# A change to the first attention of a two-block transformer kernel: item order, head-pair values, and who loads and masks the bias

## The reference, cut to what matters

```python
def neighbourhood_attention(x, w_qkv, w_o, rpb):
    qkv = (x @ w_qkv).reshape(b, rows, GRID_W, 3, N_HEADS, HEAD_DIM)   # rows = 4, GRID_W = 64
    ...
        sc = jnp.einsum('bhqd,bhrkd->bhqrk', qi, kr).astype(jnp.float32)
        sc = sc + jnp.transpose(bias, (0, 2, 1, 3))[None]
        sc = jnp.where(col_mask[:, None, :], sc, NEG_INF)
        p = jax.nn.softmax(...)
        return jnp.einsum('bhqrk,bhrkd->bhqd', p.astype(vr.dtype), vr)
    ...
    return o @ w_o
```

## Time and profile before

| what | value |
|---|---|
| median of 3 runs | 2100.27 us (2098.11 to 2106.24) |
| profiled execution, span from first to last instruction | 2099.1 us |
| TensorE busy | 1917.0 us, 91% |
| VectorE busy | 1000.8 us, 48% |
| ScalarE busy | 644.8 us, 31% |
| GpSimd busy | 217.1 us, 10% |
| mean granted TensorE clock | 0.943 |

### The profile page before, as it was taken

How to read it: one execution, slowest core, us unless ns; L and a number is a source line. 1 busy time by engine, 2 the same in 40 slices (tenths; PEclk the granted TensorE clock), 3 DMA queues, 4 the chain that set the end, 5 groups by cost and what they waited for, 6 DMA issues and landing times.

```text
span 2099.1 us, 33697 instructions
## 1 busy us (share of the span) xinstructions
PE 1917.0 (91%) x14454; PEld 1390.5 (66%) x14454; DVE 1000.8 (48%) x1382; ACT 644.8 (31%) x1004; POOL 217.1 (10%) x218
## 2 busy tenths in 40 slices
PE   6878999899997899989999779989899999999993
PEld 5757999889996899855765669874344444444440
DVE  4664554555654677756545774663122121111116
ACT  4334333544444533330033531422111111111110
POOL 0000000000000100002100014401111121121213
PEclk9878999999999999999899879989999999999996
DMA  9313555544442777546511000066998998998886
GB/s 328 101 61 114 190 188 180 168 152 153 150 151 91 263 248 250 162 150 193 160 51 43 0 13 4 3 274 269 386 381 341 379 382 347 379 371 353 329 344 256
DMA packets 191893, 438.68 MB, mean 209 GB/s; under 512 B 24208, under 2 KB 145552, under 8 KB 162448
## 3 DMA queue, kind: packets, MB, share of 16 engines
q1 hardware_dynamic: 156336, 352.02, 45.6%
q0 software_dynamic: 23040, 43.05, 6.0%
q10 hardware_dynamic: 12384, 41.69, 5.1%
HBM read 501.68 MB, written 26.21 MB: 251 GB/s over the span
## 4 chain that ended last, share of the span: by engine, by line
PE 79%; DVE 10%; DMA 4%; ACT 3%; issue 2%; SPq 0%; POOL 0%; ACTq 0%; DVEq 0%; POOLq 0%
PE psum L344 30%; PE psum L3324 15%; PE psum L3345 7%; PE psum L1538 7%; PE psum L3295 4%; PE psum L1545 2%; DMA mem<-in_exp_w_dram 2%; PE psum L2555 2%; ACT w_hi L400 1%; DMA mem<-in_na_w_qkv_dram 1%; PE psum L2539 1%; DVE w_lo L405 1%; DVE mem L3449 1%; PE psum L564 1%; PE psum L3085 1%
## 5 line engine op out<-in xcount | busy, mean ns | idle before, releaser
L405 DVE TENSOR_TENSOR w_lo<-mem,w_hi 128x2048 fp32r<-128x2048 f32 x122 | 279.3, 2291 | 264.6 <-ACT w_hi L400 262.0
L344 PE MATMUL psum<-x_hi,w_hi 128*128 128x256 f32 x1216 | 352.0, 289 | 4.5 <-DVE x_lo L551 4.5
L3324 PE MATMUL psum<-mem 128*64 128x512 f32 x1536 | 342.4, 599 | 9.5 <-DMA mem<-in_exp_w_dram 9.4
L344 PE MATMUL psum<-x_hi,w_lo 128*128 128x256 f32 x1216 | 346.1, 285 | 0.0
L344 PE MATMUL psum<-x_lo,w_hi 128*128 128x256 f32 x1216 | 345.3, 284 | 0.0
L400 ACT ACTIVATE w_hi<-mem 128x2048 fp32r<-128x2048 f32 x122 | 233.8, 1918 | 199.7 <-PE psum L344 186.1
L3324 PEld LDWEIGHTS psum<-mem 128*64 128x64 f32 x1536 | 110.6, 138 | 233.2 <-issue 214.6
L344 PEld LDWEIGHTS psum<-x_hi,w_hi 128*128 128x128 f32 x1216 | 235.8, 194 | 11.1 <-DVE w_lo L405 4.9
L344 PEld LDWEIGHTS psum<-x_lo,w_hi 128*128 128x128 f32 x1216 | 239.3, 197 | 0.7
L344 PEld LDWEIGHTS psum<-x_hi,w_lo 128*128 128x128 f32 x1216 | 238.1, 196 | 0.0
L3345 PE MATMUL psum<-mem 128*64 128x512 f32 x768 | 177.0, 603 | 1.2 <-DVE mem L3396 1.0
(11 more groups left out here) (494 smaller groups left out, 2963.4 us busy)
## 6 DMA issues: line engine op xcount, KB each, us to landing
mem<-in_exp_w_dram SPq DMA_DIRECT2D x192, 1024.0 KB, 12.5
mem<-in_dil_w_qkv_dram SPq DMA_DIRECT2D x36, 1024.0 KB, 5.3
mem<-in_ada_w_dram POOLq DMA_DIRECT2D x48, 512.0 KB, 4.7
y_rows<-mem ACTq DMA_DIRECT2D x48, 512.0 KB, 8.0
mem<-in_ffn_w_gate_dram SPq DMA_DIRECT2D x22, 1024.0 KB, 5.6
mem<-in_ffn_w_up_dram SPq DMA_DIRECT2D x22, 1024.0 KB, 5.6
mem<-in_ffn_w_down_dram SPq DMA_DIRECT2D x22, 1024.0 KB, 4.8
mem<-in_w_in_dram SPq DMA_DIRECT2D x13, 1024.0 KB, 5.6
```

What stands on the lines that cost most here:

```text
L344: ins = pe.matmul(out, lhs[a], rhs[b], start=start and k == 0, stop=stop and k == 2, **kw)
L405: dve.tensor_tensor(w_lo[n % SLOTS][:, 0, :], ring[:, n % SLOTS, :], w_hi_f[n % HI][:, 0, :], ALU.subtract).then_inc(S("w_split"), 1)
L3324: ins = pe.matmul(psum[r, up, :].rearrange("p (a n) -> p a n", a=2), xg[:, b % 2, c, x * P + 64 * e:x * P + 64 * e + 64], w_up[s][e][:, :, ...
```

## The change

- The items come in another order: head blocks 2 and 3 first get Q and K each, and then V of both.
- The units start at slots 4, 5, 7, 8, 10, 11, 13, 14, 16, 17, 18, ..., 23: one in each slot from 16 on.
- The value products of a pair of heads (two units) are made together, in 8 matmuls, in slots 8, 11, 14, 17, 22, 23, 24 and 26; their output leaves PSUM in one copy of 256 columns. The list of slots ends at 26.
- The turned probabilities have six buffers in place of two, and ScalarE copies them out of PSUM in place of VectorE.
- `lo_dve` moves from the end of a slot of the second half to the end of the next one, behind that slot's `scaled` and `biased`.
- The bias is loaded in four quarters, the first ahead of the attention, the others from ScalarE's queue after slots 1, 5 and 9, each behind a wait for the one before. The constants follow after slot 11, the gain row after slot 15, the small inputs after slot 17.
- The mask is added to the bias on GpSimd, a quarter at a time.

```diff
@@ -775,10 +775,11 @@
 
 
 
+    PT_RING = 6
     qT, kT, v_tok = alloc(KC, SEQ), alloc(KC, SEQ), alloc(NT, D)
     na_bias = alloc(HEADS, 6, GRID_W)
     na_p = alloc(2, 2, SEQ)
-    na_pT = alloc(2, 4, P)
+    na_pT = alloc(PT_RING, 4, P)
     na_s = alloc(2, 2, SEQ)
     na_max = alloc(2 * HEADS)
     na_sum = alloc(2 * HEADS)
@@ -814,10 +815,12 @@
 
         eng.wait_ge(S(f"qkv_moved{m % 2}"), m // 2 + 1)
 
-    NA_ITEMS = [(hb, kind) for hb in range(4) for kind in range(3)]
+    NA_ITEMS = [(0, 0), (0, 1), (0, 2), (1, 0), (1, 1), (1, 2), (2, 0), (2, 1), (3, 0), (3, 1), (2, 2), (3, 2)]
+    NA_AT = {item: m for m, item in enumerate(NA_ITEMS)}
     PAIRS2 = HEADS
-    NA_START = [6 * (q // 4) + 5 + (0, 1, 3, 4)[q % 4] for q in range(PAIRS2)]
-    NA_SLOTS = range(NA_START[-1] + 4)
+    NA_START = [4, 5, 7, 8, 10, 11, 13, 14, 16, 17, 18, 19, 20, 21, 22, 23]
+    NA_VALUES = [max(NA_START[2 * j + 1] + 3, 2 * NA_AT[j // 2, 2] + 2 + j % 2) for j in range(KC)]
+    NA_SLOTS = range(NA_VALUES[-1] + 1)
 
     def heads2(q):
 
@@ -840,8 +843,8 @@
 
         def scores(q):
             hb, hp, t = heads2(q)
-            moved(pe, 3 * hb)
-            moved(pe, 3 * hb + 1)
+            moved(pe, NA_AT[hb, 0])
+            moved(pe, NA_AT[hb, 1])
             if q >= 2:
                 pe.wait_ge(*at("na_biased", q - 1))
             for x in range(2):
@@ -859,17 +862,17 @@
                     ins = pe.transpose(bank(4, P, (2 * x + kc) * P), na_p[:, q % 2, x, kc * P:(kc + 1) * P], ident)
             ins.then_inc(S("na_turned"), 1)
 
-        def values(q):
-            hb, hp, t = heads2(q)
-            pe.wait_ge(*at("na_pT", q + 1))
-            moved(pe, 3 * hb + 2)
-            if q:
-                pe.wait_ge(*at("na_o", q))
-            for kc in range(2):
-                for x in range(2):
-                    h = 4 * hb + 2 * hp + x
-                    ins = pe.matmul(psum[HD * x:HD * x + HD, 5, 0:P], v_tok[:, kc, h * HD:(h + 1) * HD],
-                                    na_pT[:, q % 2, 2 * x + kc, :], start=kc == 0, stop=kc == 1)
+        def values(j):
+            pe.wait_ge(*at("na_pT", 2 * j + 2))
+            moved(pe, NA_AT[j // 2, 2])
+            if j:
+                pe.wait_ge(*at("na_o", j))
+            for t in range(NT):
+                for kc in range(2):
+                    for x in range(2):
+                        h = 2 * j + x
+                        ins = pe.matmul(bank(5, P, t * P)[HD * x:HD * x + HD, :], v_tok[:, kc, h * HD:(h + 1) * HD],
+                                        na_pT[:, (2 * j + t) % PT_RING, 2 * x + kc, :], start=kc == 0, stop=kc == 1)
             ins.then_inc(S("na_pv"), 1)
 
         for s in NA_SLOTS:
@@ -882,10 +885,11 @@
                 ins = product(m, half, w)
                 if half == 1:
                     ins.then_inc(S("item_used"), 1)
+            for j in range(KC):
+                if s == NA_VALUES[j]:
+                    values(j)
             for q in range(PAIRS2):
-                if s == NA_START[q] + 3:
-                    values(q)
-                elif s == NA_START[q] + 2:
+                if s == NA_START[q] + 2:
                     turn(q)
                 elif s == NA_START[q]:
                     scores(q)
@@ -910,28 +914,40 @@
                 act.activation(na_p[:, q % 2, x, :], na_s[:, q % 2, x, :], ACT.Exp, bias=na_max[:, u:u + 1],
                                accum_out=na_sum[:, u:u + 1]).then_inc(S("na_exp"), 1)
 
+        def turned(q):
+            act.wait_ge(*at("na_turned", q + 1))
+            if q >= PT_RING:
+                act.wait_ge(*at("na_pv", (q - PT_RING) // 2 + 1))
+            act.activation(na_pT[:, q % PT_RING], bank(4).rearrange("p (a b) -> p a b", a=4), ACT.Copy
+                           ).then_inc(S("na_pT"), 1)
+
         for s in NA_SLOTS:
             m, half = divmod(s, 2)
             if half == 1 and m < len(NA_ITEMS) and m % 2 == 0:
                 dst, src, f = na_move(act, m)
                 act.activation(dst, src, ACT.Copy, scale=f).then_inc(S("qkv_moved0"), 1)
+            for j in range(KC):
+                if s == NA_VALUES[j]:
+                    act.wait_ge(*at("na_pv", j + 1))
+                    act.activation(oT[:, j, :], bank(5, SEQ), ACT.Copy).then_inc(S("na_o"), 1)
             for q in range(PAIRS2):
-                if s == NA_START[q] + 3:
-                    hb, hp, t = heads2(q)
-                    act.wait_ge(*at("na_pv", q + 1))
-                    act.activation(oT[:, 2 * hb + hp, t * P:(t + 1) * P], bank(5, P), ACT.Copy).then_inc(S("na_o"), 1)
+                if s == NA_START[q] + 2:
+                    turned(q)
                 elif s == NA_START[q]:
                     exp(q)
             if half == 1 and m < len(NA_ITEMS):
                 hi_act(act, NA_QKV + m + HI)
+                if m in (0, 2, 4):
+                    bias_load(act, m // 2 + 1)
+                elif m == 5:
+                    act.wait_ge(S("na_bias_in"), 16 * 5)
+                    act.dma_start(cst[:, P:], d["cst"][:, P:]).then_inc(S("na_bias_in"), 16)
+                elif m == 7:
+                    gain_load(act, g_row("norm_mix_post", 0), 0)
+                elif m == 8:
+                    mod_inputs(act)
 
     def na_dve(dve):
-
-        def bias(hb):
-            if hb == 0:
-                dve.wait_ge(S("na_bias_in"), 48)
-            b = na_bias[:, 4 * hb:4 * hb + 4].rearrange("p h j k -> p (h j) k")
-            dve.tensor_tensor(b, b, bc(na_window, 1, 24), ALU.add).then_inc(S("na_bias_ready"), 1)
 
         def biased(q):
             hb, hp, t = heads2(q)
@@ -961,20 +977,25 @@
                 dst, src, f = na_move(dve, m)
                 dve.tensor_scalar(dst, src, f, None, ALU.mult).then_inc(S("qkv_moved1"), 1)
             for q in range(PAIRS2):
-                if s == NA_START[q] + 2:
-                    dve.wait_ge(*at("na_turned", q + 1))
-                    if q >= 2:
-                        dve.wait_ge(*at("na_pv", q - 1))
-                    dve.tensor_copy(na_pT[:, q % 2], bank(4).rearrange("p (a b) -> p a b", a=4)
-                                    ).then_inc(S("na_pT"), 1)
-                elif s == NA_START[q] + 1:
+                if s == NA_START[q] + 1:
                     scaled(q)
                 elif s == NA_START[q]:
                     biased(q)
-            if half == 1 and m < len(NA_ITEMS):
-                lo_dve(dve, NA_QKV + m + HI)
-                if m % 3 == 1:
-                    bias(m // 3)
+            if half == 0 and 1 <= m <= len(NA_ITEMS):
+                lo_dve(dve, NA_QKV + m - 1 + HI)
+        dve.wait_ge(S("na_bias_in"), 16 * 6)
+
+    def bias_load(act, hb):
+        if hb:
+            act.wait_ge(S("na_bias_in"), 16 * (hb + 1))
+        act.dma_start(na_bias[:, 4 * hb:4 * hb + 4].rearrange("p h j k -> p (h j k)"),
+                      d["rpb_rows"][:, 24 * GRID_W * hb:24 * GRID_W * (hb + 1)]).then_inc(S("na_bias_in"), 16)
+
+    def na_pool(pool):
+        for hb in range(4):
+            pool.wait_ge(S("na_bias_in"), 16 * (hb + 2))
+            b = na_bias[:, 4 * hb:4 * hb + 4].rearrange("p h j k -> p (h j) k")
+            pool.tensor_tensor(b, b, bc(na_window, 1, 24), ALU.add).then_inc(S("na_bias_ready"), 1)
 
 
     DIL_ITEMS = [(hb, g, kind) for hb in range(4) for kinds in ((0, 1), (2,)) for g in range(GROUPS) for kind in kinds]
...
@@ -1255,13 +1276,10 @@
         rms_hi_act(act, gains[:, 0, :], 6)
         hi_act(act, NA_QKV + 1)
         act.dma_start(na_window, d["na_window"]).then_inc(S("na_bias_in"), 16)
-        act.dma_start(na_bias.rearrange("p h j k -> p (h j k)"), d["rpb_rows"]).then_inc(S("na_bias_in"), 16)
+        bias_load(act, 0)
         hi_act(act, NA_QKV + EARLY)
-        act.dma_start(cst[:, P:], d["cst"][:, P:]).then_inc(S("na_bias_in"), 16)
-        gain_load(act, g_row("norm_mix_post", 0), 0)
-        mod_inputs(act)
         na_act(act)
-        o_split_act(act, "na_o", NA_WO)
+        o_split_act(act, "na_o", (6, 8), NA_WO)
         residual_act(act, NA_WO + 4)
         rms_root_act(act)
         gain_load(act, g_row("norm_ffn_post", 0), 1)
@@ -1278,7 +1296,7 @@
         rms_hi_act(act, gains[:, 1, :], 6, True)
         hi_act(act, DIL_QKV + EARLY)
         dil_act(act)
-        o_split_act(act, "dil_o", DIL_WO)
+        o_split_act(act, "dil_o", (12, 16), DIL_WO)
         residual_act(act, DIL_WO + 4)
         rms_root_act(act)
         gain_load(act, g_row("norm_ffn_post", 1), 3)
@@ -1321,6 +1339,7 @@
 
     def block1_pool(pool):
 
+        na_pool(pool)
         pool.wait_ge(S("x_split"), X_NO["dil"] + KC)
         for dst, src in ((xw_hi, x_hi), (xw_lo, x_lo)):
             pool.tensor_copy(dst[:, :, 0:HD], src[:, :, 3 * HD:]).then_inc(S("x_wrapped"), 1)
```

(8 more changed lines are left out.)

## The result

The changed kernel runs in 2069.97 us (median of 4, 2066.02 to 2073.08), the kernel before in 2100.4 (median of 4). The ratio is 0.9838 with a 95% interval of 0.9819 to 0.9857: 30.4 us less. Five more runs gave 2068.62, ratio 0.9842 (0.9818 to 0.9866). The forecast was 2066.

What follows compares the result with a forecast made beforehand. TensorE's gaps in the attention, waiting for a late VectorE and slowing the clock, were taken as the bound. The walk put the first projection product at 128.3 against 162.65, -34.35 us: span 2064.75, plus 1.2 gives 2066, range 2059 to 2070.

Steps and rivals of the forecast that it cites:

- Units and slots: TensorE's walk through the attention: half products at 3.03 or 2.83 us, slots 5 to 23 sum 78.1, last half ends at 111.7.
- Early transfers: Attention's start: with a quarter of the bias alone ahead, ScalarE's 6.8 us wait for item 3 goes; no term of its own.
- Is VectorE late?: Dense slots 16 to 23: VectorE needs 4.35 us a slot against TensorE's 4.5, just keeps up; cost nothing, otherwise 2.4 us.
- Rival A: VectorE becomes the pace of the attention's dense slots: about 6 to 12 us more, 2072 to 2078; chance 0.14.
- Is ScalarE late?: Dense slots: with the copy of turned probabilities ScalarE needs 3.0 of 4.5 us; the copy is wanted a slot later; cost nothing.
- ScalarE's waits for the quarters: Behind slots 5, 9 and 11 ScalarE waits for the bias quarter issued 15, 12 and 11 us before; cost nothing.
- Rival C: Slower, by ScalarE's three waits for bias quarters in the attention: 41.3 us at the longest landing seen, 2107; chance 0.02.
- Mask on GpSimd: Attention: each add about 3.4 us, may hold up VectorE by 0 to 13.6 in all; taken as 1.0 us.
- Tail: From the last half at 111.7 to the first projection product at 127.3, or 128.3 with the mask's 1.0: 15.6 us.
- Sum: Attention stage shorter by 34.35 us, coming through whole: span 2099.1 to 2064.75, plus 1.2 for the median, 2066.
- Rival D: Gain given back later, as feed-forward items might not be loaded in time: at most 2 x 6.9 us, 2080; chance 0.03.
- Rival B: Only the attention's tail is won, the body's last half still ends at 129.6: 17.5 us less, 2083; chance 0.04.

Runs made afterwards that it cites:

- e10: Changed kernel with the bias in one load, constants, gain row and small inputs ahead of the attention, and the mask adds on VectorE; attention stage 115.9 us.
- e1: Changed kernel with the four mask adds back on VectorE, at slots 3, 9, 15 and 19; attention stage 108.9 us.
- e3: Changed kernel with the copy of the turned probabilities back on VectorE, ring of six kept; attention stage 110.2 us.
- r_before: Kernel before, unedited, profiled again: first output projection product at 163.37 us, span behind it 1940.9 against 1936.5.
- e6: Kernel before with only the four bias loads, the mid-stage constants and the mask on GpSimd; attention stage 137.9 us, 8.1 less than before.
- e4: Changed kernel with the units' old starts and value products three slots behind a pair's second unit, last at slot 30; attention stage 117.8 us.

## Why the prediction was right, step by step

- *Units and slots.* Forecast 111.7 for the end of the last half, 1.0 more with the mask; measured 111.68 and, in the second profile, 112.13. The products cost 3.01 to 3.03 and 2.83 as priced; a pair's values are 1.02, not 1.18, which gave back 0.8 in five; the first five halves ended 0.6 early; the one wait took 1.34.
- *Early transfers.* Item 3 was rounded at 25.13 without a wait, forecast 25.7. That the step has no term of its own agrees with the walk, but it hid its worth: e10 against e1 puts 6.9 us on it, close to the 6.7 that the prediction gave as the most.
- *Is VectorE late?* Mis-sized. I had it at 4.35 us a slot with nothing left. With 0.69 more for each unit (e3) the body has no wait above 0.4, and with 1.75 more once in the dense slots (e1) none: the copy fits into the wait for the exponentials, 1.16 before it and 0.46 behind. The 4.35 holds 1.1 us of that waiting in every second slot, in which a copy has room. Rival A is out.
- *Is ScalarE late?* Waits of TensorE for the new copy on ScalarE were named as a sign of being wrong, and the 5.6 us that are left are all for it: 3.6 and 0.7 in the tail, where the walk had them, and 1.34 in the body, where the mask's 1.0 comes due through ScalarE's copy. The walk had the copy at nothing because of the six buffers; but bank 4 holds one turned unit, so the next turn needs the copy a slot later all the same.
- *ScalarE's waits for the quarters.* Landed in 4.4 to 7.3 us, where a stall needs over 11. Rival C is out.
- *Mask on GpSimd.* The price of 1.0 holds for this kernel (1.34 as a wait, 1.0 to 1.8 by e1), but as a cost with nothing on the other side. I had counted the mask among the things that leave VectorE and so help. The length of an add was priced at 3.4, and one that meets no item difference takes 3.49; the mean of 4.4 holds the time in which VectorE holds GpSimd. That the lock is dear when the adds come in one row (6.4 us) I hadn't priced at all.
- *Tail.* 14.7 and 15.1 against 15.6. The chain was as walked; the turn behind ScalarE's copy, priced at 1.1, took 0.64 in one profile and 1.10 in the other, and the last values 2.0.
- *Sum.* -34.35 forecast for the stage, -36.3 and -35.4 measured in the profiles; 2066 forecast, 2069.97 and 2068.62 measured. The stage itself came out 1 to 2 us shorter than forecast, so somewhat more than the difference of the medians lies behind it. That "what it gains should come through whole" is the sentence that doesn't hold: of 35.4 to 36.3 us in the stage 30 to 32 came through in the medians. A later stage longer by more than 3 us was named as a sign of being wrong, and it came up in the first profile (the stretch of the second block, 3.2 longer than before) and not in the second. R was 8.4 and 3.1 longer in the two profiles of the change than in the first of before, and 4.5 longer in r_before with nothing edited. It goes with the granted clock in later serial stretches, and the prediction had no term for that; that the time still fell into the forecast is in part luck. Rival D's cause, late items, isn't seen: the feed-forward layer took 197.7 us against 197.4.
- *Rival B* is out with the body at 111.7.

What stays open: taken away one at a time, the starts are worth 7.9, the order 3.0, the loads 6.9, the copy on ScalarE 0.2 or less, the mask less than nothing. That is 17 of 36, and such shares needn't add up. Between e6 (137.9) and e4 (117.8) lie 20 us, 15 in the body and 5 in the tail, that belong to the order, the copy on ScalarE, the ring of six, the values by pair and the later place of `lo_dve` together. The last three weren't tried alone. From the lists I would argue for the place of `lo_dve`, as a 2.29 us operation no longer stands ahead of short ones; that is argued, not shown.

## What to carry to other kernels

Walk the bounding engine through its own list with prices from dense rows, and only ask of the others whether they are a slot late; here that gave the end of a 95 us stretch to within 1 us. Where a tail is a chain through one engine's list, reorder that list: rounding for later work ahead of a copy that is waited for, and a split that could be made in parts, were worth 7 us together. Before moving an elementwise operation to GpSimd to relieve VectorE, look whether VectorE is on the path at all, and don't queue several there in one row beside differences and divisions of VectorE for which something waits.

## What the runs showed of the hardware

- GpSimd and VectorE hold each other up for a whole instruction, both ways. A GpSimd add took 3.49 us with no item difference under way and 5.49 with one; a VectorE item difference took 5.49 in place of 2.29, and a pair of divisions 6.81 in place of 0.62. Operations with a PSUM input and the maximum kept their 0.69. The Trainium skill (SBUF — State Buffer, "Who interferes with whom") has both the exclusive lock and this exemption, and the runs agree.
- An unchanged kernel's later serial stretch comes in two lengths, 41.8 and 45.0 us, with the granted clock at 0.80 and 0.70. A few microseconds of a 2100 us program can't be judged by its total; a stage is judged by its own start and end.
